# Attention's output with the values as weights, in a two-layer hybrid transformer step on one core

## The chip, the core and the metric

The kernel runs on one core of one Trainium2 chip, written instruction by instruction in Bass: TensorE multiplies, VectorE, ScalarE and GpSimd work beside it, and SyncE issues nearly all the DMA transfers. The metric is the device time of one execution, in microseconds (us). In the profile PE is TensorE's matmul, PEld its weight load, DVE VectorE, ACT ScalarE, POOL GpSimd, and SP or SPq SyncE and its queue. A matmul has two operands: the one that lies in the array (the weights, its columns become the partitions of the result) and the one that streams through it (its columns become the columns of the result). The result lies in PSUM, here in eight banks of 128 partitions by 512 fp32 numbers, ps0 to ps7.

## What is computed

Two layers work on 128 context tokens (b = 0) and 128 latent tokens (b = 1). This case changes only the attention's last step. Cut to what matters:

```python
# D_MODEL 1024, 8 query heads over 2 key/value heads (R = 4), head_dim 64
def one_block(qblk):
    s = jnp.einsum('bqgrd,bkgd->bgrqk', qblk, k).astype(jnp.float32) * scale
    p = jax.nn.softmax(s, axis=-1).astype(v.dtype)
    return jnp.einsum('bgrqk,bkgd->bqgrd', p, v)
...
# latent tokens: k, v = 128 cached keys and 128 own; context tokens: 128 own keys
x = x + gt1 * (jnp.concatenate([att, ml], axis=-1) @ w_out)
...
x = x + gt2 * _moe(h, ...)        # 16 experts, top 2, gate/up/down of 1024 x 512
```

The softmax's division is done last: the kernel computes the sum of exp(score) times value, and divides by the sum of exp(score) of the row.

## The kernel before

All weights (some 289 MB of traffic) are streamed from HBM once, in loads of 2 MB, into ten places in SBUF: a ring of seven, two places called `beside` and one called `over`. SyncE issues them in one written order, and each load waits until the instruction that read the place's last contents is done. In each layer TensorE's program is: norm and projections (L764, L778), the transposes of keys and queries, scores, the parallel mLSTM heads, attention, the output projection in four quarters `mix` 0 to 3 (L1014), the router, and eight pairs of experts (`into_hidden` L1100, `down` L1130), 64 matmul instructions in each of three blocks of a pair.

The order on each engine is the order of the code. A PSUM bank is handed on by a plan, `bank_plan`: every result has a key, `begin(key)` makes TensorE wait until the bank's last contents were read, `full(engine, key)` makes a reader wait until the result is there, and `free(key)` tells that it was read. Attention's results take banks 4, 5 and 6 in turn, in the order in which they are listed; `shiftdot` (a small product for the router, L994) comes into bank 5 behind them.

The steps around the change, in each layer:

- TensorE's weighted sums, L969 (b = 1, over cached keys and own keys) and L976 (b = 0). The exponentials (`pT1`, `pT0`, keys on partitions, 128 queries as columns) are the weights, and the values `cv` and `vx` stream, 64 numbers and a 1 behind them: so the 65th column is the divisor, on the same partition as its query. Bank keys `o10`, `o11`, `o00`, `o01`.
- VectorE's `attended(b)`: a reciprocal of the four divisors of a half (L1840) and a multiplication of 128x256 (L1841) into `on`, twice for each b.
- TensorE's mLSTM state products (L984, keys `C`), a transpose of the state's n (L990), `shiftdot` (L994), then `turn_heads` (L909), eight transposes that turn the attention output so that the heads' columns lie on partitions, and eight of the mLSTM output (L1002, keys `mlT`). ScalarE copies the turned heads from PSUM into `cat` (L1487), the operand of the output projection.
- VectorE between them: `heads_out(1)` ends with L1810, then `attended(1)`, the output gate's product (L1869, two of 128x512), `attended(0)`, the head norm's product (L1874, two of 128x512; `ml_ready`, for which L1002 waits), and the copy of n (L1877).
- SyncE: the first two loads into `beside` wait for key `o01`. The first into `over` waits until the layer's states are written out, the last of them a small transfer from L1877's copy.
- GpSimd loads the next layer's state and cache when `o11` is there.

Of the kernel before, what the change touches and what calls it, by code (L numbers as in the profile page):

```python
# [22 lines left out]
ALU = mybir.AluOpType  # L23
# [3 lines left out]
P = 128  # L27
# [105 lines left out]
def bank_plan():  # L133
# [17 lines left out]
    for l in range(DEPTH):  # L151
# [33 lines left out]
        for k in ("qT1", "kT1", "qT0", "kT0", "s10", "s11", "s12", "s13", "s00", "s01",  # L185
                  "p10", "p11", "p12", "p13", "p00", "p01", "o10", "o11", "o00", "o01", "oT1", "oT0"):
            att(k)
# [85 lines left out]
def build(nc, t):  # L273
    banks, weights = bank_plan(), weight_plan()
    with ExitStack() as ctx:
# [26 lines left out]
        cv = sb("cv", [P, NKV, HD + 1])  # L302
        vx = sb("vx", [P, NB, NKV, HD + 1])
# [4 lines left out]
        shares = sb("shares", [P, NB, NQ])  # L308
# [40 lines left out]
        on = qkr[:, :, 0:NQ * HD]  # L349
# [146 lines left out]
        def _(sp):  # L496
# [56 lines left out]
            for l in range(DEPTH):  # L553
# [57 lines left out]
        def _(pe):  # L611
# [121 lines left out]
            for l in range(DEPTH):  # L733
# [170 lines left out]
                def turn_heads(b):  # L904

                    bank = begin((f"oT{b}", l))
                    taken(pe, (f"o{b}0", l), (f"o{b}1", l))
                    for j in range(4):
                        mm = pe.transpose(bank[:, j * P:(j + 1) * P], on[:, b, j * P:(j + 1) * P], ident)  # L909
                    done((f"oT{b}", l), mm)  # L910
# [51 lines left out]
                for g in range(NKV):  # L962
                    bank = begin((f"o1{g}", l))
                    taken(pe, (f"p1{2 * g}", l), (f"p1{2 * g + 1}", l))
                    for n in range(4):
                        j, par = n // 2, n % 2
                        for kb in range(2):
                            v = cv[:, g, :] if kb == 0 else vx[:, 1, g, :]
                            mm = pe.matmul(bank[:, n * (HD + 1):(n + 1) * (HD + 1)], pT1[:, 2 * g + par, j, kb, :], v,  # L969
                                           start=(kb == 0), stop=(kb == 1))  # L970
                    done((f"o1{g}", l), mm)
                taken(pe, ("p00", l), ("p01", l))
                for g in range(NKV):
                    bank = begin((f"o0{g}", l))
                    for n in range(4):
                        mm = pe.matmul(bank[:, n * (HD + 1):(n + 1) * (HD + 1)], pT0[:, n % 2, 2 * g + n // 2, :], vx[:, 0, g, :],  # L976
                                       start=True, stop=True)
                    done((f"o0{g}", l), mm)
# [17 lines left out]
                turn_heads(1)  # L996
                turn_heads(0)
# [6 lines left out]
                taken(pe, ("oT1", l), ("oT0", l))  # L1004
# [270 lines left out]
        def _(act):  # L1275
# [69 lines left out]
            for l in range(DEPTH):  # L1345
# [138 lines left out]
                for b in (1, 0):  # L1484
                    key = (f"oT{b}", l)
                    bank = full(act, key)
                    act.activation(cat[:, 0:4, b * P:(b + 1) * P], bank[:, :].rearrange("p (k t) -> p k t", k=4),  # L1487
                                   ACT.Copy).then_inc(free(key), 1)
# [75 lines left out]
        def _(dve):  # L1564
# [4 lines left out]
            dve.memset(vx[:, :, :, HD:], 1.0)  # L1569
            dve.memset(cv[:, :, HD:], 1.0)  # L1570
# [87 lines left out]
            for l in range(DEPTH):  # L1658
# [87 lines left out]
                for b in range(NB):  # L1746
# [3 lines left out]
                    dve.tensor_copy(vx[:, b, :, 0:HD], bank[:, NKV * HD:2 * NKV * HD].rearrange("p (g d) -> p g d", g=NKV))\  # L1750
# [83 lines left out]
                def attended(b):  # L1834

                    for g in range(NKV):
# [4 lines left out]
                        dve.tensor_tensor(on[:, b, 4 * g * HD:4 * (g + 1) * HD].rearrange("p (n d) -> p n d", n=4), o[:, :, 0:HD],  # L1841
                                          per_col(share, HD), ALU.mult).then_inc(free(key), 1)
# [207 lines left out]
        def _(pool):  # L2050
            def layer_loads(l):
                pool.dma_start(C0[:, :, 0:MD], t["state_C"][0, l].rearrange("a h d e -> d (a h) e")).then_inc(layer_in, 16)
                pool.dma_start(ck[:, :], t["cache_k"][0, l].rearrange("s g d -> s (g d)")).then_inc(layer_in, 16)
                pool.dma_start(cv[:, :, 0:HD], t["cache_v"][0, l]).then_inc(layer_in, 16)
# [6 lines left out]
            def pool_keys(l):  # L2061
# [3 lines left out]
                pool.dma_start(t["new_cache_v"][0, l], vx[:, 0, :, 0:HD]).then_inc(kv_out, 16)  # L2065
# [18 lines left out]
            for l in range(DEPTH):  # L2084
# [21 lines left out]
                if l + 1 < DEPTH:  # L2106
                    full(pool, ("o11", l))
# [53 lines left out]
```

## Time and profile before

| | |
|---|---|
| median of 3 runs | 792.96 us (792.9 to 793.29) |
| profiled execution, its own time | 794.9 us |
| its span | 793.0 us |
| TensorE busy | 759.5 us, 96% of the span |
| VectorE, ScalarE, GpSimd busy | 329.3, 158.2, 56.6 us |
| mean of the DMA | 365 GB/s |

The span is the time from the first to the last instruction in the trace; the execution's own time has about 1.9 us around it. A busy TensorE is one with an instruction in flight, not one at its peak.

### The profile page before, as it was taken

The numbers are of one execution on the slowest core, as the hardware profiler recorded it, in microseconds if no ns is written. First come the engines' busy times: TensorE is split into PE (matmuls) and PEld (weight loads), VectorE is DVE, ScalarE is ACT, GpSimd is POOL, SyncE is SP. The second block draws the span as 40 slices with busy tenths as digits, with TensorE's granted clock in tenths as the row PEclk, the third lists the DMA queues.
The fourth block names the chain that finished last, engine by engine and source line by source line (L and its number), as shares of the span: only waits on it lengthen the run. The fifth ranks groups of instructions, "written<-read, shape, count | busy, mean of one in ns | idle before, by whom it ended". The sixth has DMA issues, their size and how long they took to land.

```text
span 793.0 us, 10913 instructions
## 1 busy us (share of the span) xinstructions
PE 759.5 (96%) x4683; PEld 401.3 (51%) x4683; DVE 329.3 (42%) x534; ACT 158.2 (20%) x355; POOL 56.6 (7%) x69
## 2 busy tenths in 40 slices
PE   3799999999999999999899999999899999999997
PEld 2265556786534433444245646688653444344423
DVE  0279566714323232123228965772431323213223
ACT  2301114602212012020012111361221201102001
POOL 0040052101100000000000004200110000000000
PEclk9999999999999999999999999999999999999999
DMA  8999907999999999999999970579889999999993
GB/s 346 403 378 374 375 7 295 413 362 424 426 420 424 423 421 425 426 419 423 422 407 407 380 301 0 218 289 397 326 328 400 427 426 418 424 426 419 426 421 152
DMA packets 49858, 289.41 MB, mean 365 GB/s; under 512 B 3401, under 2 KB 5761, under 8 KB 23697
## 3 DMA queue, kind: packets, MB, share of 16 engines
q1 hardware_dynamic: 48080, 285.30, 88.6%
q0 software_dynamic: 1488, 3.31, 1.2%
q8 instruction: 39, 0.64, 0.3%
q10 hardware_dynamic: 240, 0.08, 0.0%
q14 instruction: 11, 0.08, 0.0%
HBM read 286.31 MB, written 2.37 MB: 364 GB/s over the span
## 4 chain that ended last, share of the span: by engine, by line
PE 83%; DMA 13%; DVE 2%; SPq 1%; ACT 1%; issue 0%; ACTq 0%; DVEq 0%
PE ps L1100 22%; PE ps L764 16%; PE ps L1130 12%; DMA ring<-in_w_e_up 9%; PE ps L1014 7%; PE ps L1084 4%; DMA ring<-in_w_in 4%; PE ps L778 4%; PE ps L639 3%; PE ps L1145 2%; PE ps L1112 1%; PE ps L1155 1%; PE ps L892 1%; PE ps L917 1%; PE ps L947 1%; DVE xT L1654 1%
## 5 line engine op out<-in xcount | busy, mean ns | idle before, releaser
L1100 PE MATMUL ps<-ring,xe 128*64 128x512 f32 x688 | 151.8, 594 | 4.0 <-DMA ring<-in_w_e_up 4.0
L764 PE MATMUL ps<-ring,hT 128*128 128x512 f32 (+1 forms) x320 | 128.7, 564 | 2.0 <-DMA ring<-in_w_in 2.0
L1100 PEld LDWEIGHTS ps<-ring,xe 128*64 128x64 f32 x688 | 48.5, 137 | 105.3 <-issue 99.8
L764 PEld LDWEIGHTS ps<-ring,hT 128*128 128x128 f32 x320 | 62.1, 196 | 65.2 <-issue 59.5
L1130 PE MATMUL ps<-ring,ex 128*32 128x512 f32 x736 | 92.0, 594 | 0.2 <-issue 0.2
L1995 DVE COPY ye<-ps 64x512 f32<-64x512 f32 (+1 forms) x28 | 19.3, 689 | 164.2 <-PE ps L1130 164.1
L1014 PE MATMUL ps<-hT,ring 128*128 128x256 f32 x256 | 57.1, 381 | 0.0
L1979 DVE RECIPROCAL ex<-ex 128x512 f32<-128x512 f32 x16 | 53.6, 3353 | 0.6
L1130 PEld LDWEIGHTS ps<-ring,ex 128*32 128x32 f32 x736 | 26.0, 110 | 52.1 <-issue 49.4
L1977 DVE TENSOR_SCALAR ex<-ex 128x512 f32<-128x512 f32 x16 | 6.8, 427 | 109.4 <-ACT ex L1528 109.4
L1014 PEld LDWEIGHTS ps<-hT,ring 128*128 128x128 f32 x256 | 48.0, 190 | 7.2 <-issue 0.8
L1100 PE MATMUL ps<-beside,xe 128*64 128x512 f32 x208 | 46.2, 594 | 0.0
L1528 ACT ACTIVATE ex<-ps 128x512 f32<-128x512 f32 x16 | 9.6, 597 | 143.4 <-PE ps L1100 143.4
L1130 PE MATMUL ps<-beside,ex 128*32 128x512 f32 x224 | 35.3, 594 | 2.0 <-issue 2.0
L1678 DVE SCALAR_TENSOR_TENSOR pT<-ring,cT,pT 128x2048 f32<-128x2048 f32 x14 | 32.9, 2348 | 5.6 <-DMA ring<-in_w_mod 5.6
L1678 DVE SCALAR_TENSOR_TENSOR sideways<-ring,cT,sideways 128x2048 f32<-128x2048 f32 x14 | 32.9, 2347 | 0.0
L1084 PEld LDWEIGHTS ps<-lists,hT 128*128 128x128 f32 x256 | 29.7, 192 | 5.8 <-issue 4.9
L639 PE MATMUL ps<-ring,cT 128*32 128x512 f32 (+1 forms) x320 | 31.6, 525 | 0.6 <-DMA ring<-in_w_mod 0.6
L1084 PE MATMUL ps<-lists,hT 128*128 128x128 f32 x256 | 31.6, 278 | 0.1
L1544 ACT ACTIVATE ye<-ps 64x512 f32<-64x512 f32 (+1 forms) x28 | 16.6, 592 | 68.7 <-PE ps L1130 68.6
L1521 ACT ACTIVATE xe<-ps 128x512 f32<-128x512 f32 x32 | 19.1, 597 | 54.0 <-PE ps L1084 54.0
L1100 PEld LDWEIGHTS ps<-beside,xe 128*64 128x64 f32 x208 | 14.6, 137 | 30.0 <-issue 29.9
(272 smaller groups left out, 803.6 us busy)
## 6 DMA issues: line engine op xcount, KB each, us to landing
ring<-in_w_mod SPq DMA_DIRECT2D x24, 2048.0 KB, 19.1
ring<-in_w_e_up SPq DMA_DIRECT2D x23, 2048.0 KB, 20.0
ring<-in_w_e_gate SPq DMA_DIRECT2D x20, 2048.0 KB, 22.3
ring<-in_w_e_down SPq DMA_DIRECT2D x19, 2048.0 KB, 23.2
ring<-in_w_in SPq DMA_DIRECT2D x10, 2048.0 KB, 23.4
beside<-in_w_e_gate SPq DMA_DIRECT2D x8, 2048.0 KB, 25.5
beside<-in_w_e_down SPq DMA_DIRECT2D x7, 2048.0 KB, 19.8
beside<-in_w_e_up SPq DMA_DIRECT2D x5, 2048.0 KB, 18.1
```

The lines of the kernel that those rows point to most:

```text
L639: mm = pe.matmul(bank[32 * g:32 * g + 32, 0:width], cT[:, c:c + 32], w[:, k, g * width:(g + 1) * width], start=(c == 0), stop=(c == NB * ( ...
L764: mm = pe.matmul(bank[:, 0:width], hT[:, k, b * P:(b + 1) * P], w[:, k, :], start=(k == 0), stop=(k == KD - 1))
L778: mm = pe.matmul(bank[:, j * TOK:(j + 1) * TOK], w[:, k, h * MD:(h + 1) * MD], hT[:, k, :], start=(k == 0), stop=(k == KD - 1))
L1014: mm = pe.matmul(bank[:, j * TOK:(j + 1) * TOK], w[:, k, c:c + P], cat[:, k, :], start=(k == 0), stop=(k == KD - 1))
L1084: mm = pe.matmul(bank[:, c:c + P], htok[:, b, 2 * i + k, :], pick[:, b, 4 * q:4 * q + 4, :].rearrange("p e c -> p (e c)"), start=True, sto ...
L1100: mm = pe.matmul(bank[PLACES * j:PLACES * j + PLACES, :], xe[:, k, c:c + PLACES], w[:, j, i, :], start=(k == 0), stop=(k == KD - 1))
L1130: mm = pe.matmul(bank[32 * g:32 * g + 32, :], hidT[:, k, c:c + SLOTS], w[j][:, k, half * 512:(half + 1) * 512], start=(k == 0), stop=(k == ...
L1521: act.activation(xe[:, 2 * i:2 * i + 2, :].rearrange("p k (e b s) -> p b (k e) s", e=4, b=NB), bank[:, :].rearrange("p (b n s) -> p b n s" ...
L1544: ins = act.activation(ye[r, plane, 0:512], bank[r, :], ACT.Copy)
L1678: ins = dve.scalar_tensor_tensor(modsum[b], w[:, k % 2, :], one, modsum[b], ALU.mult, ALU.add)
L1979: dve.reciprocal(ex[:, :], ex[:, :]).then_inc(silu_step, 1)
L1995: ins = dve.tensor_copy(ye[r, plane, 512:1024], bank[r, :])
```

## The change

For each b and each of the two key/value heads the values are now the weights (64 columns) and the exponentials of two query heads stream (256 columns). The result has the head's 64 numbers on partitions and the queries as columns, which is the form that `cat` wants. Even query heads go to partitions 0 to 63 and odd ones to 64 to 127. The same products with ones instead of values give the divisors, the same number on all 64 partitions, in a second bank (`d1`, `d0`). The divisors are therefore 128x512 numbers where they were 128x4 four times over (two of these reciprocals for each b). The transposes `turn_heads` and their banks go, with ScalarE's two copies. VectorE multiplies from PSUM straight into `cat`. `attended(0)` moves behind the head norm's product.

```diff
-                  "p10", ... "p01", "o10", "o11", "o00", "o01", "oT1", "oT0"):
+                  "p10", ... "p01", "o1", "d1", "o0", "d0"):
...
-                                full(sp, ("o01", l))
+                                full(sp, ("d0", l))
...
+                def over_keys(key, blocks, parts):
+                    bank = begin((key, l))
+                    for g in range(NKV):
+                        for i, part in enumerate(parts):
+                            for par in range(2):
+                                v = blocks[i][:, g, :] if blocks else ones[:, 0:HD]
+                                mm = pe.matmul(bank[64 * par:64 * par + 64, g * TOK:(g + 1) * TOK], v, part(g, par),
+                                               start=(i == 0), stop=(i == len(parts) - 1))
+                    done((key, l), mm)
...
+                over_keys("o1", (cv, vx[:, 1]), both)
+                over_keys("d1", None, both)
                 taken(pe, ("p00", l), ("p01", l))
+                over_keys("o0", (vx[:, 0],), own_keys)
...                                     # the state products C
+                over_keys("d0", None, own_keys)
                 filling(6, 7)
...                                     # nT, shiftdot
-                turn_heads(1)
-                turn_heads(0)
...
 def attended(b):
-                    for g in range(NKV):
-                        key = (f"o{b}{g}", l)
-                        o = full(dve, key)[:, 0:4 * (HD + 1)].rearrange("p (n d) -> p n d", n=4)
-                        share = shares[:, b, 4 * g:4 * g + 4]
-                        step(dve.reciprocal(share, o[:, :, HD]))
-                        dve.tensor_tensor(on[...], o[:, :, 0:HD], per_col(share, HD), ALU.mult).then_inc(free(key), 1)
+                    key = (f"d{b}", l)
+                    bank = full(dve, key)
+                    dve.reciprocal(share[:, b, :], bank[:, :]).then_inc(free(key), 1)
+                    taken(dve, key)
+                    key = (f"o{b}", l)
+                    bank = full(dve, key)
+                    dve.tensor_tensor(cat[:, 0:4, b * P:(b + 1) * P], bank[:, :].rearrange("p (k t) -> p k t", k=4),
+                                      share[:, b, :].rearrange("p (k t) -> p k t", k=4), ALU.mult).then_inc(free(key), 1)
...
                 for b in range(NB):
                     note(dve.tensor_tensor(o[b], o[b], mqT[:, b, :, :], ALU.mult))
-                attended(0)
                 dve.wait_ge(head_rstd, l + 1)
                 settle()
                 for b in range(NB):
                     dve.tensor_tensor(o[b], o[b], per_col(hr[:, b, :], MD), ALU.mult).then_inc(ml_ready, 1)
+                attended(0)
```

Three places of the program follow, the same in both layers. A row is one instruction or a run of equal ones (x3): line, operation, result and operands, size of the result, and the semaphores it waits for (one fp32 matmul here is two instructions in the trace); `bank_read5` is "the last contents of bank 5 were read", `bank_full5` "the result in bank 5 is there". Lines are those of each kernel's own file.

TensorE before, the end of the weighted sums: the last products of b = 1 (`cv` cached, `vx` own values, streaming) and all those of b = 0.

```order
L969 MATMUL ps6<-cv,pT1 128x65
L969 MATMUL ps6<-vx,pT1 128x65
L976 MATMUL ps4<-vx,sideways 128x65 [waits bank_read4,bank_read6]
L976 MATMUL ps4<-vx,sideways 128x65 x3
L976 MATMUL ps5<-vx,sideways 128x65 [waits bank_read5]
L976 MATMUL ps5<-vx,sideways 128x65 x3
```

TensorE now, all but one of the new groups: `o1` in ps5, `d1` in ps6 (with `ones`), `o0` in ps4.

```order
L910 MATMUL ps5<-pT1,cv 64x256 [waits bank_read4,bank_read6,bank_read5,bank_read1,bank_read0]
L910 MATMUL ps5<-pT1,cv 64x256
L910 MATMUL ps5<-pT1,vx 64x256 x2
L910 MATMUL ps5<-pT1,cv 64x256 x2
L910 MATMUL ps5<-pT1,vx 64x256 x2
L910 MATMUL ps6<-pT1,ones 64x256 [waits bank_read6]
L910 MATMUL ps6<-pT1,ones 64x256 x7
L910 MATMUL ps4<-sideways,vx 64x256 [waits bank_read4,bank_read6]
L910 MATMUL ps4<-sideways,vx 64x256 x3
```

Sixteen products of 128x65 and eight behind them became eight, eight and four of 64x256.

TensorE before, from the last of the state products to the transposes of the mLSTM output; `wr,modc` is `shiftdot`, `cst,qkr` the turned heads, `cst,og` the mLSTM output.

```order
L984 MATMUL ps1<-mv,kw 128x129 [waits bank_read1]
L984 MATMUL ps1<-mv,kw 128x129
L990 MATMUL ps2<-cst,qk 8x128 [waits bank_read1,bank_read2]
L994 MATMUL ps5<-wr,modc 2x16 [waits bank_read5]
L994 MATMUL ps5<-wr,modc 2x16 x7
L909 MATMUL ps6<-cst,qkr 128x128 [waits bank_read6,bank_read5]
L909 MATMUL ps6<-cst,qkr 128x128 x3
L909 MATMUL ps4<-cst,qkr 128x128 [waits bank_read5,bank_read4]
L909 MATMUL ps4<-cst,qkr 128x128 x3
L1002 MATMUL ps3<-cst,og 128x128 [waits ml_ready,bank_read3]
L1002 MATMUL ps3<-cst,og 128x128 x3
```

TensorE now, at the same place.

```order
L976 MATMUL ps1<-mv,kw 128x129 [waits bank_read1]
L976 MATMUL ps1<-mv,kw 128x129
L910 MATMUL ps5<-sideways,ones 64x256 [waits bank_read5]
L910 MATMUL ps5<-sideways,ones 64x256 x3
L983 MATMUL ps2<-cst,qk 8x128 [waits bank_read1,bank_read2]
L987 MATMUL ps5<-wr,modc 2x16 [waits bank_read5]
L987 MATMUL ps5<-wr,modc 2x16 x7
L993 MATMUL ps3<-cst,og 128x128 [waits ml_ready,bank_read3]
L993 MATMUL ps3<-cst,og 128x128 x3
L993 MATMUL ps0<-cst,og 128x128 [waits ml_ready,bank_read0]
L993 MATMUL ps0<-cst,og 128x128 x3
```

The eight transposes are gone. `d0` has come in behind the state products and needs bank 5 read, whose contents are now `o1`; `shiftdot` needs bank 5 read as before, and its contents are now `d0`.

VectorE before, from the end of the mLSTM's sum to the product for which the transposes of `og` wait.

```order
L1840 RECIPROCAL shares<-ps5 128x4 [waits bank_full5]
L1841 TENSOR_TENSOR qkr<-ps5,shares 128x256 [waits dve_step]
L1840 RECIPROCAL shares<-ps6 128x4 [waits bank_full6]
L1841 TENSOR_TENSOR qkr<-ps6,shares 128x256 [waits dve_step]
L1869 TENSOR_TENSOR og<-og,mqT 128x512 [waits head_sum]
L1869 TENSOR_TENSOR og<-og,mqT 128x512
L1840 RECIPROCAL shares<-ps4 128x4 [waits bank_full4]
L1841 TENSOR_TENSOR qkr<-ps4,shares 128x256 [waits dve_step]
L1840 RECIPROCAL shares<-ps5 128x4 [waits bank_full5]
L1841 TENSOR_TENSOR qkr<-ps5,shares 128x256 [waits dve_step]
L1874 TENSOR_TENSOR og<-og,hr 128x512 [waits dve_step,head_rstd]
```

VectorE now, at the same place; `qkr` is where the reciprocals `share` lie, `hT` is `cat`.

```order
L1822 RECIPROCAL qkr<-ps6 128x512 [waits bank_full6]
L1826 TENSOR_TENSOR hT<-ps5,qkr 128x4x128 [waits bank_full5,bank_read6]
L1854 TENSOR_TENSOR og<-og,mqT 128x512 [waits head_sum]
L1854 TENSOR_TENSOR og<-og,mqT 128x512
L1858 TENSOR_TENSOR og<-og,hr 128x512 [waits dve_step,head_rstd]
L1858 TENSOR_TENSOR og<-og,hr 128x512
L1822 RECIPROCAL qkr<-ps5 128x512 [waits bank_full5]
L1826 TENSOR_TENSOR hT<-ps4,qkr 128x4x128 [waits bank_full4,bank_read5]
L1862 COPY nst<-ps2 8x128 [waits bank_full2]
```

Four pairs of a small reciprocal and a multiplication became two pairs of 128x512, and the second pair now stands behind both products with `hr`. Bank 5 as `shiftdot` needs it (`d0` read) is given by the second 128x512 reciprocal.

## Rows read from the trace of the kernel before

**Rows 1.** The page: shares of the last chain, two groups of instructions

```profile
PE 83%; DMA 13%; DVE 2%; SPq 1%; ACT 1%; issue 0%; ACTq 0%; DVEq 0%
L1100 PE MATMUL ps<-ring,xe 128*64 128x512 f32 x688 | 151.8, 594 | 4.0 <-DMA ring<-in_w_e_up 4.0
L1979 DVE RECIPROCAL ex<-ex 128x512 f32<-128x512 f32 x16 | 53.6, 3353 | 0.6
```

**Rows 2.** Stretch, length, busy of PE, PEld, DVE, ACT, POOL; PEclk, DMA share, GB/s

```profile
170.00:175.00 5.00, 5.00 (x30) 4.01 (x29) 1.13 (x4) 0.63 (x1) 0.00 (x0) 1.00 0.74 298
530.00:535.00 5.00, 4.43 (x50) 3.97 (x49) 3.08 (x9) 2.90 (x9) 1.47 (x2) 1.00 0.77 267
585.00:590.00 5.00, 5.00 (x26) 1.71 (x24) 0.00 (x0) 0.02 (x1) 0.00 (x0) 1.00 0.51 164
610.00:730.00 120.00, 120.00 (x786) 51.33 (x786) 31.32 (x28) 18.38 (x32) 0.00 (x0) 1.00 1.01 423
```

**Rows 3.** SyncE's timeline: start, us to the last issue, what

```profile
174.13 0.37 SPq L579 DMA_DIRECT2D over<-in_w_e_up  x1
...
175.06 12.89 SPq L584 DMA_DIRECT2D ring<-in_w_e_down  x2
193.74 2.78 SPq L579 DMA_DIRECT2D ring<-in_w_e_gate  x2
...
530.16 0.37 SPq L579 DMA_DIRECT2D beside<-in_w_e_gate  x1
...
586.54 0.34 SPq L584 DMA_DIRECT2D ring<-in_w_e_down  x1
```

**Rows 4.** The chain in order of time, around the change: start, us, what

```profile
147.47 3.52 PE ps L969 x32
150.99 1.79 PE ps L976 x16
152.77 1.85 PE ps L984 x16
...
155.45 0.48 PE ps L994 x16
155.93 1.03 PE ps L909 x8
156.96 0.87 PE ps L1002 x8
157.83 7.06 PE ps L1014 x32
...
532.75 0.48 PE ps L994 x16
```

**Rows 5.** The same chain, stretches that give rates of TensorE

```profile
34.14 15.70 PE ps L764 x32
...
65.86 27.66 PE ps L764 x64
...
231.47 13.88 PE ps L1100 x64
```

**Rows 6.** VectorE's timeline around attended: start, us, what

```profile
150.09 0.69 DVE L1810 TENSOR_TENSOR mqT<-work 128x512 f32<-128x512 f32 x1
...
150.91 0.42 DVE L1841 TENSOR_TENSOR qkr<-ps,shares 128x256 f32<-128x256 f32 x1
...
151.80 1.28 DVE L1869 TENSOR_TENSOR og<-og,mqT 128x512 f32<-128x512 f32 x2
...
154.10 1.28 DVE L1874 TENSOR_TENSOR og<-og,hr 128x512 f32<-128x512 f32 x2
...
528.28 0.18 DVE L1840 RECIPROCAL shares<-ps 128x4 f32<-128x4 f32 x1
```

**Rows 7.** Two stretches of 2 us before and in a slow clock

```profile
32.00:34.00 2.00, 0.15 (x1) 0.00 (x0) 1.96 (x5) 1.36 (x5) 0.00 (x0) 1.00 1.05 432
...
36.00:38.00 2.00, 2.00 (x3) 0.72 (x3) 0.00 (x0) 0.00 (x0) 0.00 (x0) 0.50 1.00 392
```

More of the change, by code:

```diff
@@ L185, in bank_plan @@
         for k in ("qT1", "kT1", "qT0", "kT0", "s10", "s11", "s12", "s13", "s00", "s01",
-                  "p10", "p11", "p12", "p13", "p00", "p01", "o10", "o11", "o00", "o01", "oT1", "oT0"):
+                  "p10", "p11", "p12", "p13", "p00", "p01", "o1", "d1", "o0", "d0"):
             att(k)
@@ L301, in build @@
         ck = sb("ck", [P, NKV * HD])
-        cv = sb("cv", [P, NKV, HD + 1])
-        vx = sb("vx", [P, NB, NKV, HD + 1])
+        cv = sb("cv", [P, NKV, HD])
+        vx = sb("vx", [P, NB, NKV, HD])
         rstd = sb("rstd", [P, TOK])
@@ L307, in build @@
         peaks = sb("peaks", [P, NB, NQ])
-        shares = sb("shares", [P, NB, NQ])
         dn = sb("dn", [P, NB, MH, 2])
@@ L348, in build @@
         gl = prob[:, 18 * P:20 * P]
-        on = qkr[:, :, 0:NQ * HD]
+        share = qkr[:, :, 0:NQ * HD]
         inter_s = hT.ap().rearrange("p k t -> p (k t)")[:, MH * TOK:MH * TOK + 6 * (MD + 1)].rearrange("p (n d e) -> p n d e", n=3, d=2)
@@ L902, in carried @@
                     done((("inter", h), l), mm)
[L904 to L910, printed above, removed]
+                def over_keys(key, blocks, parts):
[7 more added lines that the diff above has]
+                    done((key, l), mm)
                 def cross_scores(i):
@@ L961, in _ @@
                 taken(pe, (("akv", 0), l), (("akv", 1), l))
-                for g in range(NKV):
[L963 to L971, printed above, removed]
-                taken(pe, ("p00", l), ("p01", l))
[L973 to L978, printed above, removed]
+                both = [lambda g, par, kb=kb: pT1[:, 2 * g + par, :, kb, :] for kb in range(2)]
+                own_keys = [lambda g, par: pT0[:, par, 2 * g:2 * g + 2, :]]
+                taken(pe, *[(f"p1{i}", l) for i in range(4)])
+                over_keys("o1", (cv, vx[:, 1]), both)
+                over_keys("d1", None, both)
+                taken(pe, ("p00", l), ("p01", l))
+                over_keys("o0", (vx[:, 0],), own_keys)
                 pe.wait_ge(kw_ready, 2 * (l + 1))
@@ L1003, in _ @@
                     done((("mlT", b), l), mm)
-                taken(pe, ("oT1", l), ("oT0", l))
+                taken(pe, ("o1", l), ("o0", l))
                 fill = last_section(l)
@@ L1483, in _ @@
                                    bank[:, 0:2 * (MD + 1)].rearrange("p (d e) -> p d e", d=2), ACT.Copy).then_inc(free(key), 1)
[L1484 to L1488, printed above, removed]
                 key = (("mlT", 0), l)
@@ L1749, in _ @@
                     dve.tensor_copy(qk[:, b, NQ * HD:], bank[:, 0:NKV * HD])
-                    dve.tensor_copy(vx[:, b, :, 0:HD], bank[:, NKV * HD:2 * NKV * HD].rearrange("p (g d) -> p g d", g=NKV))\
+                    dve.tensor_copy(vx[:, b, :, :], bank[:, NKV * HD:2 * NKV * HD].rearrange("p (g d) -> p g d", g=NKV))\
                         .then_inc(free(key), 1)
@@ L1834, in attended @@
                 def attended(b):
-                    for g in range(NKV):
-                        key = (f"o{b}{g}", l)
-                        o = full(dve, key)[:, 0:4 * (HD + 1)].rearrange("p (n d) -> p n d", n=4)
-                        share = shares[:, b, 4 * g:4 * g + 4]
-                        step(dve.reciprocal(share, o[:, :, HD]))
-                        dve.tensor_tensor(on[:, b, 4 * g * HD:4 * (g + 1) * HD].rearrange("p (n d) -> p n d", n=4), o[:, :, 0:HD],
-                                          per_col(share, HD), ALU.mult).then_inc(free(key), 1)
+                    key = (f"d{b}", l)
[6 more added lines that the diff above has]
+                                      share[:, b, :].rearrange("p (k t) -> p k t", k=4), ALU.mult).then_inc(free(key), 1)
                 dve.wait_ge(layer_in, 16 * LAYER_LOADS * (l + 1))
@@ L2053, in layer_loads @@
                 pool.dma_start(ck[:, :], t["cache_k"][0, l].rearrange("s g d -> s (g d)")).then_inc(layer_in, 16)
-                pool.dma_start(cv[:, :, 0:HD], t["cache_v"][0, l]).then_inc(layer_in, 16)
+                pool.dma_start(cv[:, :, :], t["cache_v"][0, l]).then_inc(layer_in, 16)
             def gate_weights(l):
@@ L2106, in _ @@
                 if l + 1 < DEPTH:
-                    full(pool, ("o11", l))
+                    full(pool, ("o1", l))
                     full(pool, (("inter", MH - 1), l))
```

4 lines of the change are left out of this document (1 added, 3 removed).

## The prediction, made before the changed kernel had run

> **What bounds the kernel now.** I read the chain of work that ended last first, because a busy share is no bound. Its shares are 83% TensorE and 13% DMA, and the reader should see that the two alternate: the DMA comes in at the end of each layer's experts, and the group of L1100 waited 4.0 us in all for `e_up` weights [rows 1]. So I looked at the DMA's stretches. From 610 to 730 us, in the experts, it moves 423 GB/s at a share of 1.01: full, and a load of 2.1 MB takes 2.1 / 423 = 4.96 us there. Where it is not full is what decides: 0.74 from 170 to 175 us, 0.77 from 530 to 535, 0.51 from 585 to 590 [rows 2]. SyncE's timeline says why: loads are issued in order when a place comes free, and those at 193.74 and 586.54 us waited for TensorE's own progress [rows 3]. A TensorE that comes later to the output projection issues these loads later by as much, and from there to the layer's end the DMA has no pause in which to catch up. Both bounds therefore move with TensorE's lateness in this stretch, and the question is only when the output projection (L1014) starts: at 157.83 us in layer 0 [rows 4].
>
> **What ends the wait there.** In the chain around the change there is hardly an idle time: weighted sums 3.52 and 1.79 us, state products 1.85, `shiftdot` at 155.45, turned heads 1.03, mLSTM output 0.87 [rows 4]. VectorE runs beside it, close behind: `heads_out(1)` starts its last instruction at 150.09 and takes 0.69, a multiplication of 128x256 takes 0.42, the two products with the gate 1.28 and the two with the norm 1.28 [rows 6]. It has no slack of microseconds to give.
>
> **TensorE's own work.** Removed per layer: 3.52 + 1.79 + 1.03 = 6.34 us [rows 4]. Added: 8 + 8 + 4 + 4 products of 64x256. The trace has none of this form. The nearest is L1100, 64-column weights in alternating halves of the array: 64 instructions of 512 columns in 13.88 us, 0.217 each, against 27.66 for 64 full-width ones, 0.432 [rows 5]. Half the columns gives 0.108; a product is two instructions, so 24 x 0.217 = 5.2 us. The other bound is that the halves don't overlap: 0.441, from L1014's 7.06 us for 16 products of 256 columns [rows 4], or 10.6 us. The new products alternate halves just as L1100 does, so I take 5.2: TensorE saves 1.1 us per layer in work.
>
> **VectorE's work.** Removed per layer: four multiplications of 0.42 and four small reciprocals of 0.18 [rows 6], 2.4 us. Added: two reciprocals of 128x512 and two multiplications of 128x512. The reciprocal of that size takes 3353 ns [rows 1]; the multiplication 0.64, half of 1.28 [rows 6]. That is 8.0 us. The row reads SBUF and the new one PSUM; the small reciprocals from PSUM show no penalty at 0.18, so I keep 3.35. The Trainium skill ("VectorE: DVE Perf Modes", "First, the fixed hardware budget") says a reciprocal iterates with a repeat count of 8; at the clock of 0.96 GHz that the page gives, 512 x 8 cycles would be an estimated 4.3 us, and the stalls below would be 3.7 us longer in all. The measured 3353 ns speaks against it, though for another source.
>
> **The new wait, layer 0.** o1 and d1 are 16 products: from 147.47, 3.5 us, so d1 is there at about 151.2 with the end of its pipeline, and VectorE, done at 150.8, waits until then. Then in its order: reciprocal 3.35, multiplication 0.64, gate 1.28, norm 1.28, reciprocal 3.35, in sum 9.9, to 161.1 us. `shiftdot` needs bank 5, now held by d0 until that second reciprocal has read it. So it starts at 161.1 instead of 155.45: 5.65 late. Behind it on TensorE stand the mLSTM transposes and the output projection, without the turned heads' 1.03: 4.6 us late. Before that TensorE also waits some 1.6 us for bank 5 ahead of d0 (o1 is read at 155.2; o0 and the state products end near 153.7); this is inside the 4.6, not added to it. The order of VectorE that puts the norm ahead of `attended(0)` gives nothing back, because the mLSTM transposes stand behind `shiftdot`. `over`'s first load, which waits for L1877's copy and a transfer [rows 3], is behind the same reciprocal, but the next layer's state is loaded 1.7 us earlier (o1 ends earlier than the last of L969); I count nothing.
>
> **Layer 1.** Here VectorE came to `attended(1)` at 528.28 [rows 6] and d1 is there at the same time: TensorE's way from the sums to `shiftdot` is 8.0 us in layer 0, so here it began at 524.8 or before and has d1 by 528.5. 528.28 + 9.9 = 538.2, against `shiftdot` at 532.75 [rows 4]: 5.45, less 1.03, 4.4 us late. The first load into `beside`, at 530.16 [rows 3], goes to d0's end, some 3 us later, and the DMA stands idle so much longer; but it was idle again from 585 to 590 [rows 2] for a load that waits on TensorE, so those 3 us are inside TensorE's lateness.
>
> **The clock.** From 32 to 34 us TensorE was busy 0.15 of 2 us, and from 36 to 38 us its granted clock is 0.50, the 1.2 GHz level [rows 7]; the first 32 instructions behind that pause took 15.70 us where 32 take 13.83 [rows 5]: 1.87 us lost. The new stalls leave it nearly idle for 6.3 of 7.4 us (153.7 to 161.1). I therefore expect a fall in both layers. Its price is at least what falls on the dense output projection, 1.9; it may take the eight transposes too (0.87 [rows 4], doubled), giving 2.8. I take 2.0 per layer, near the measured pause. The Trainium skill ("TensorE: Matmul & The Clock Gate", "What you observe") states the same rule, that activity releases the throttle and a pause brings it back; by it alone the sum has these 4.0 us, without it 4.0 less.
>
> **What hides some of it.** In layer 0 the DMA has a short queue when `e_gate` is issued at 193.74. Three loads were issued by 175.1 [rows 3], the DMA was dry shortly before (0.74 [rows 2]) and starts on them near 176; with 3 x 4.96 they end at 190.9, and the one issued at 187.95 (175.06 + 12.89) ends at 195.9. From issue to bytes a load needs at least 1.0 us (issued at 530.16 into an idle DMA, and the share of 530 to 535 is 0.77, so bytes flow from 531.2 or later [rows 2, 3]). So 193.74 was early by 1.2 us at most. That is all the cover; I take 0.5.
>
> **The sum.** Layer 0: 4.6 + 2.0 - 0.5 = 6.1. Layer 1: 4.4 + 2.0 = 6.4. Together 12.5 us on the profiled execution's 794.9, which is 1.9 above the median of 793.0: **805.5 us**.
>
> **The rivals.**
> - *No fall of the clock.* The few products inside the stall keep it up; short pauses elsewhere cost nothing. Then 8.5 us: 801.5. Against it: rows 7, with a shorter pause. 0.17.
> - *The stream hides it.* TensorE waited 4.0 us for `e_up` [rows 1], so up to 2 us per layer of lateness could be free: 801.5 with the fall, 797.5 without. It needs loads that don't wait for TensorE, and rows 3 has them waiting at both places. 0.08.
> - *The halves don't overlap.* 16 products for o1 and d1 take 7.1 instead of 3.5, VectorE starts 3.5 later in layer 0 and 3 in layer 1: 812. 0.06.
> - *The skill's slow reciprocal*, 4.3 us: 809. 0.03.
> - *Faster.* The 128x512 reciprocal is cheap. The lateness is two reciprocals less what went, 2r - 2.0 in layer 0 and 2r - 2.2 in layer 1; at r = 1.0 us it is nothing, and at the multiplication's 0.64 TensorE's 1.1 us of saved work counts: 791. For it: nothing but that the row has another source. 0.04, with the no change near r = 1.
> - My forecast: 0.62.
>
> **Numbers.** 800.5 to 810 leaves out the faster case, half of the stream's, the halves' and some of the tails, some 0.18. A measurement of this kernel tells 0.2%, 1.6 us, from nothing. Slower by more: all but the last rival and a little of the second, 0.95; same 0.02; faster 0.03.
>
> **What would show it.** Right: a wait of TensorE of over 4 us before the 2x16 products of `shiftdot`, ended by VectorE's reciprocal of 128x512 from PSUM at 3.3 us; the output projection starting 4.5 to 8 us after 157.83; a granted clock of 0.5 just behind the stall in both layers; the load after 193.74 late by as much; the chain passing through VectorE in both layers. Wrong: a reciprocal under 2 us, a clock that stays at 1.00, or pauses before the last pair's weights shrinking by more than 1 us per layer.

## The result, and the profile after

The changed kernel takes **805.03 us** (median of 4 runs, 803.31 to 807.03) against 792.93 for the kernel before on the same chip: a ratio of 1.0151, interval 1.0135 to 1.0168. It is 12.1 us slower, where 12.5 was forecast. Its profiled execution took 803.31 us, with a span of 801.5.

The first lines are the page of the changed kernel: busy times, then the chain that ended last.

```profile
PE 756.4 (94%) x4660; PEld 395.7 (49%) x4667; DVE 341.2 (43%) x524; ACT 155.7 (19%) x351; POOL 55.9 (7%) x69
...
PE 81%; DMA 12%; DVE 4%; SPq 1%; issue 1%; ACT 1%; DVEq 0%; ACTq 0%
```

TensorE is busy 3 us less than before and the kernel is slower: it waits more. (Those 3 us are no measure of the work saved. Slow stretches of the clock count in them, and the two profiles have theirs in different places.) VectorE's share of the chain is 4%, against 2% before, and TensorE's 81%, against 83% [rows 1]. Where VectorE came in is seen in the chain of layer 0's stretch of the change (start us, us, what; "x" counts instructions).

```profile
144.70 3.63 PE ps L910 x32
...
148.35 3.37 DVE qkr L1822
...
151.74 0.69 DVE hT L1826
152.44 1.21 DVE og L1854 x2
...
154.35 0.68 DVE og L1858
155.03 3.28 DVE qkr L1822
...
158.36 0.59 PE ps L987 x16
158.94 1.90 PE ps L993 x8
160.84 7.42 PE ps L1005 x32
```

Read against [rows 4], where nearly every step was TensorE's: from the end of the products for o1 and d1 (148.33) to `shiftdot` (L987, 158.36) every step is VectorE's, but for some 0.6 us of short gaps between them. Its two reciprocals of 128x512 (L1822) make 6.65 of the 10.0 us. Layer 1 has the same tail:

```profile
531.24 3.36 DVE qkr L1822
...
537.91 3.28 DVE qkr L1822
...
541.23 0.59 PE ps L987 x16
541.82 1.90 PE ps L993 x8
```

TensorE's own timeline shows the two waits in brackets, with what ended each:

```profile
152.49 1.08 PE L910 MATMUL ps<-sideways,ones 128*64 128x256 f32 x8 [1.34 <-DVE hT L1826]
...
158.36 0.59 PE L987 MATMUL ps<-wr,modc 128*2 128x16 f32 x16 [4.58 <-DVE qkr L1822]
```

The clock is in the windows (us, then busy us of PE, PEld, DVE, ACT, POOL, the granted clock, the DMA's share, GB/s):

```profile
154.00:156.00 2.00, 0.00 (x0) 0.00 (x0) 2.00 (x3) 0.00 (x0) 0.00 (x0) 0.73 0.99 369
156.00:158.00 2.00, 0.00 (x0) 0.00 (x0) 2.00 (x1) 0.00 (x0) 0.00 (x0) 0.50 1.03 399
158.00:160.00 2.00, 1.64 (x22) 1.59 (x23) 1.18 (x3) 0.00 (x0) 0.64 (x1) 0.50 1.01 422
160.00:162.00 2.00, 2.00 (x8) 1.79 (x8) 1.12 (x4) 1.63 (x5) 0.80 (x2) 0.56 1.01 422
162.00:164.00 2.00, 2.00 (x12) 1.74 (x11) 0.01 (x1) 0.00 (x0) 0.00 (x0) 1.00 1.01 420
...
538.00:540.00 2.00, 0.00 (x0) 0.00 (x0) 2.00 (x1) 0.00 (x0) 0.00 (x0) 0.50 0.99 311
540.00:542.00 2.00, 0.77 (x17) 0.71 (x18) 1.97 (x3) 0.00 (x0) 0.00 (x0) 0.50 0.97 410
542.00:544.00 2.00, 2.00 (x10) 1.91 (x10) 0.34 (x2) 1.10 (x5) 0.51 (x1) 0.50 1.03 434
544.00:546.00 2.00, 2.00 (x11) 1.77 (x10) 0.88 (x4) 0.32 (x2) 0.00 (x0) 0.99 0.99 422
```

The idle TensorE falls to the 1.2 GHz level in both layers and stays there through the small products behind the wait. In layer 0 it keeps that level into the output projection, whose first quarter takes 7.42 us; in layer 1 only to its first instructions (7.13 us). The load behind that projection is late too. It is issued at 197.11 (SyncE's timeline; its equal before at 193.74 [rows 3]), which is 6.1 us late, not 3.4, when both are counted from the same point, as below:

```profile
197.11 0.38 SPq L578 DMA_DIRECT2D ring<-in_w_e_gate  x1
```

**How spans are compared.** The profile of before had a clock fall of its own at 96 to 100 us, in the first layer's projections (granted 0.70 and 0.50), which this one has not. The chains of before and of the changed kernel show its price for the same 64 instructions, 1.7 us:

```profile
96.57 22.52 PE ps L764 x64
95.49 20.84 PE ps L763 x64
```

Another 1.1 us between the two had come up ahead of that. So every time after it is 2.8 us ahead of before's: the first product `mv,W` of the parallel heads starts at 128.05, before's at 130.81. I therefore measure from that product, in each layer, and call the time from it to the output projection's first product the *way*. (In layer 1 the same product starts it.)

| us | way, layer 0 | to the next norm's sums | to TensorE's first work of layer 1 | way, layer 1 | to the next norm's sums | to the last transposes |
|---|---|---|---|---|---|---|
| before | 26.94 | 57.27 | 282.78 | 25.40 | 55.52 | 276.47 |
| after | 32.59 | 63.40 | 288.65 | 30.90 | 61.21 | 282.00 |
| difference | 5.65 | 6.13 | 5.87 | 5.50 | 5.69 | 5.53 |

5.87 for layer 0 and 5.53 for layer 1 make 11.4 of the 12.1 us. All the loss is there when TensorE reaches the norm behind the output projection; what is given back behind it (0.3 and 0.2) is no more than such stretches differ from run to run.

### The profile page after: what moved, and what is told of

Its sections match the earlier page's. It is cut to its first block, busy times and chain, and to the rows that moved or that the text cites. A ratio compares the mean times of both kernels' runs of the same rounds, so it can differ in the third digit from the quotient of the medians.

```text
span 801.5 us, 10860 instructions
## 1 busy us (share of the span) xinstructions
PE 756.4 (94%) x4660; PEld 395.7 (49%) x4667; DVE 341.2 (43%) x524; ACT 155.7 (19%) x351; POOL 55.9 (7%) x69
## 3 DMA queue, kind: packets, MB, share of 16 engines
HBM read 286.31 MB, written 2.37 MB: 360 GB/s over the span
## 4 chain that ended last, share of the span: by engine, by line
PE 81%; DMA 12%; DVE 4%; SPq 1%; issue 1%; ACT 1%; DVEq 0%; ACTq 0%
PE ps L1091 22%; PE ps L763 16%; PE ps L1121 12%; DMA ring<-in_w_e_up 9%; PE ps L1005 7%; PE ps L1075 4%; PE ps L777 3%; PE ps L638 3%; DMA ring<-in_w_mod 3%; PE ps L1136 2%; DVE qkr L1822 2%; PE ps L1103 1%; PE ps L1146 1%; PE ps L891 1%; PE ps L690 1%
## 5 line engine op out<-in xcount | busy, mean ns | idle before, releaser
L763 PE MATMUL ps<-ring,hT 128*128 128x512 f32 (+1 forms) x320 | 125.3, 551 | 0.0
L763 PEld LDWEIGHTS ps<-ring,hT 128*128 128x128 f32 x320 | 60.2, 190 | 61.4 <-issue 58.2
```

What stands on the lines that cost most here:

```text
L763: mm = pe.matmul(bank[:, 0:width], hT[:, k, b * P:(b + 1) * P], w[:, k, :], start=(k == 0), stop=(k == KD - 1))
```

## The experiments

The theory: two reciprocals of 3.35 us hold bank 5, TensorE comes late by some 4.6 us and the clock falls on top; what is late there is late at the end. The rivals are those of the prediction: no price for the clock, a DMA stream that hides the lateness, halves that don't overlap. The kernels below ran in three groups on one chip each; the ratio is to the kernel before in the same group.

| label | median us | before | ratio (95%) |
|---|---|---|---|
| e1_flat | 792.1 | 792.75 | 0.9992 (0.998 to 1.0003) |
| e2_warm | 804.44 | 792.75 | 1.0148 (1.0125 to 1.0171) |
| e3_late0 | 798.41 | 792.75 | 1.0073 (1.0049 to 1.0098) |
| e4_late1 | 798.31 | 792.75 | 1.0065 (1.0044 to 1.0086) |
| e5_bank6 | 804.09 | 793.05 | 1.0135 (1.0113 to 1.0156) |
| e6_order | 805.03 | 793.05 | 1.0144 (1.0123 to 1.0165) |
| e7_beside | 792.6 | 793.05 | 0.9996 (0.9986 to 1.0007) |
| e8_scalar | 790.9 | 793.05 | 0.9979 (0.9967 to 0.9991) |
| e9_bank6_warm | 800.13 | 792.56 | 1.0103 (1.0087 to 1.0118) |
| e10_after | 804.58 | 792.56 | 1.0156 (1.0142 to 1.017) |
| e11_scalar2 | 789.22 | 792.56 | 0.9962 (0.9948 to 0.9975) |
| e12_halves | 792.44 | 792.56 | 0.9998 (0.9989 to 1.0007) |

### Without the reciprocals

```diff
-                    dve.reciprocal(share[:, b, :], bank[:, :]).then_inc(free(key), 1)
+                    dve.tensor_scalar(share[:, b, :], bank[:, :], 0.0, 0.3, ALU.mult, ALU.add).then_inc(free(key), 1)
```

> The changed kernel with the two 128x512 reciprocals of each layer replaced by a cheap operation of the same shape from the same bank into the same place (a constant 0.3 comes out, so attention's output is not divided by its sums). Theory (two reciprocals of 3.35 us each stand ahead of the read of bank 5, which shiftdot needs): the lateness per layer is two times the cheap operation's 0.7 us less 2.0 to 2.2, so the output projection starts 0.6 to 1 us earlier than in the kernel before, the clock stays at 1.00 there, and the time is 790.5 to 792.5 us. Rival A (the new products, their banks or SyncE's later wait for beside cost the time): 800 us or more. Rival B (only part is the reciprocals): 795 to 800.

Measured: 792.1 us; the whole loss is gone (with a constant in place of 1/d, so attention's output is left undivided). The two instructions take 0.70 us in the chain, in the same places:

```profile
148.37 0.70 DVE qkr L1822
...
152.30 0.70 DVE qkr L1822
...
154.62 6.91 PE ps L1005 x32
```

The ways are 26.39 and 24.70, 0.55 and 0.70 shorter than before's, and the clock stays at 1.00. So the products, their banks, the new waits and the missing transposes cost nothing; the reciprocals' length is the one cause. It also bears on the halves: had they not overlapped, this kernel would be slow too.

### The clock kept up through the wait

```diff
+                warm((("mlT", 0), l), 22)
                 bank = begin(("shiftdot", l))
```

`warm` is 22 matmuls of zeros into a bank that nobody reads yet (L690).

> The changed kernel with 22 matmuls of 128x512 in bf16 on zeros (some 4.8 us of work, into a bank that is free) ahead of shiftdot, where TensorE waits 4.6 us. Theory (the pause lets the clock fall, and that costs 1.2 to 1.5 us per layer in slow transposes and a slow begin of the output projection): granted clock 1.00 from there on, the eight transposes back at 0.9 us instead of 1.9, time 801.8 to 803 us. Rival (the fall costs nothing, all is VectorE's): 805 or more, as the added matmuls end a little after the stall.

Measured: 804.44 us (801.77 to 805.41), which the times can't tell from the changed kernel: less than expected, and as a test by the times it failed. The trace tells more. The granted clock is 1.00 throughout, and the chain shows what the same steps cost at that level:

```profile
153.45 4.76 PE ps L690 x21
158.21 0.48 PE ps L988 x16
158.69 1.02 PE ps L994 x8
159.71 6.91 PE ps L1006 x32
```

From `shiftdot` to the end of the first quarter this is 8.41 us; the changed kernel's 0.59, 1.90 and 7.42 make 9.91. At the next norm's sums it is 1.26 us ahead in layer 0 (62.14 against 63.40) and 0.97 in layer 1 (60.24 against 61.21). The ways are 31.88 and 30.20, which is 4.94 and 4.80 over before's. A part of that is the experiment's own: the added matmuls end a little after VectorE has freed bank 5 (its second reciprocal, then `shiftdot`):

```profile
154.56 3.35 DVE L1823 RECIPROCAL qkr<-ps 128x512 f32<-128x512 f32 x1
158.14 0.55 PE L988 MATMUL ps<-wr,modc 128*2 128x16 f32 x16
```

Behind the heads' first product, `shiftdot` starts at 30.47 us in layer 0 and 28.79 in layer 1, in the changed kernel at 30.31 and 28.62. Without that 0.2 us the stall alone, with the clock up, is 4.8 and 4.6, and the clock's part at the norm's sums is 1.4 and 1.1 us. At the end of each layer less of it can be seen: e2 is 0.95 ahead when layer 1 starts (287.70 against 288.65) and 0.49 at the last transposes (281.51 against 282.00). The times tell still less. The trace is of the fastest of the four runs, the only one with a mean granted clock of 1.000; the three others (803.6 to 805.4 us) have 0.997, and no trace shows where theirs fell.

### The lateness alone, in the kernel before

```diff
                 taken(pe, ("oT1", l), ("oT0", l))
+                if l == 0:
+                    warm((("mix", 0), l), 22)
```

and the same with `l == 1`: 4.76 us more ahead of the output projection in one layer, and nothing else.

> The kernel before with 22 matmuls of 128x512 in bf16 on zeros (4.8 us) ahead of the output projection, in layer 0 alone: a lateness of TensorE of known size. Theory (the weight stream waits for TensorE's progress and covers only 0.5 to 1.2 us): +3.6 to +4.3 us, 796.5 to 797.3. Rival (the stream's waits before the last pair, some 4 us, hide most of it in layer 0): +0.5 to +2.5, 793.5 to 795.5.

> The same 22 matmuls ahead of the output projection in layer 1 alone. Theory (no cover at all in layer 1, where the stream is dry between 585 and 590 us): +4.7 to +4.9 us, 797.6 to 797.9. Rival (the stream hides up to the 2 us that TensorE waits before the last pair): +2.7 to +3.5, 795.6 to 796.5.

Measured: 798.41 and 798.31 us, 5.7 and 5.6 over before. In the traces both lengthen the way by 4.80 (31.74 and 30.20). In layer 1 the last transposes come 5.05 later. In layer 0 3.9 of the 4.8 are left when layer 1 starts (286.67 against 282.78), but 4.4 at the heads' first product in layer 1 (383.28 against 378.83), and kernels that do the same up to there (e4, and e7 but for its loads) are 0.2 to 0.7 us from before over such a stretch. So by the trace 0.4 to 0.9 us of layer 0's lateness is hidden, hardly more than that spread, and by the times none; nothing is hidden in layer 1. The rival by which the stream hides the lateness is out for both. The expectations, 796.5 to 797.3 and 797.6 to 797.9, were a little low; the traces fit them better than the times. (In e3's profiled run 3.0 us of its own time lie outside the span, 1.8 to 1.9 in the others; why is open.)

### The bank of `shiftdot`

```diff
-        put(("shiftdot", l), 5)
+        put(("shiftdot", l), 6)
```

Now `shiftdot` and the mLSTM transposes run inside the wait; the output projection still needs `cat` from the second reciprocal.

> The changed kernel with shiftdot in bank 6 (read early) instead of bank 5, so that shiftdot and the eight transposes of the mLSTM output no longer wait for the second reciprocal; the output projection still waits for o0 times that reciprocal. Theory: it starts when the multiplication behind the reciprocal ends, 0.7 us after the reciprocal, instead of 0.59 + 1.90 us after it, so 1.8 us per layer are gained, time 801 to 802 us. Rival (bank 5 was the cost itself, the projection could start once it is free): 794 to 797. Rival (nothing hangs on the bank): 805.

Measured: 804.09 us, a miss. The way became 1.5 us shorter, near the 1.8 that were expected (31.07 and 29.39), but the projection gave it back:

```profile
158.84 0.82 issue
159.66 8.83 PE ps L1005 x32
```

The 0.82 us without a name are those of VectorE's multiplication into `cat`, which runs from 158.87 to 159.56. The projection's first quarter takes 8.83 us where the changed kernel needs 7.42 and a warm one 6.91, with a granted clock of 0.55 from 160 to 162 us and 0.60 from 162 to 164. TensorE is idle for 3.32 us before the projection, the fall comes later, and all of it lands on dense products. To tell whether that is the reason, 15 warm matmuls were put behind the transposes of this kernel:

```diff
+                warm((("mix", 0), l), 15)
                 taken(pe, ("o1", l), ("o0", l))
```

> shiftdot in bank 6 (as in the kernel tried before) and 15 matmuls of 128x512 in bf16 on zeros (3.25 us) in the wait ahead of the output projection. In the trace of the one without them the wait fell ahead of the projection, and the clock fell onto its dense products: from its start to the next norm 32.0 us in layer 0 instead of 30.3. Theory (the bank's 1.5 us per layer were gained and lost again to the clock): with the clock held at 1.00, 30.3 and 30.1 us for these stretches, and from the mLSTM's first product to the norm 61.3 and 59.4 us (63.4 and 61.2 in the changed kernel): 801 to 802.5 us. Rival (the bank gains nothing): 804 to 805.

Measured: 800.13 us, 4.45 less than the unedited changed kernel in the same group (e10), and a little below the 801 to 802.5 expected. The first quarter (its chain) is back at its rate, behind the same start:

```profile
155.49 3.23 PE ps L690 x14
...
158.76 7.14 PE ps L1006 x32
```

The next norm's sums come at 61.41 and 59.50, 1.7 earlier than in e5 and 2.0 and 1.7 earlier than in the changed kernel. The two parts need each other: warmth alone gave 1.3 and 1.0, the bank alone 0.3 and 0.0.

### VectorE's order, and SyncE's wait

```diff
+                attended(0)
                 dve.wait_ge(head_rstd, l + 1)
...
-                attended(0)
```

> The changed kernel with VectorE's old order: attended(0) ahead of the head norm's product again. Theory: the second reciprocal ends 1.3 us earlier, but the transposes then wait for the norm's product behind it, so only 0.2 to 0.6 us per layer are gained: 803.8 to 804.7 us. Rival (the new order is what helps, as the transposes' operand comes earlier): slower than the changed kernel, 807 or more. Rival (the new order is the cause of the loss): 800 or less.

Measured: 805.03 us, no difference that can be told. The ways are 0.45 shorter (32.14 and 30.45), which is gone again at the norm's sums (63.48 and 61.22). The clock falls here too, and later than in the changed kernel: it is at 0.50 from 160 to 164 us and still at 0.74 from 164 to 166, when the projection runs. VectorE's order is not a cause. In the kernel before, the loads into `beside` were then made to wait longer, about as the change has them wait:

```diff
                             if slot in BESIDE:
-                                full(sp, ("o01", l))
+                                full(sp, (("C", MH - 1), l))
+                                full(sp, ("oT1", l))
```

> The kernel before with SyncE's wait for the loads into beside put behind the state products and the first turned heads (some 3.8 us later in layer 1, 4 us in layer 0), nothing else changed: the changed kernel's later wait alone. Theory (the DMA is dry for that longer in layer 1, but dry again later on TensorE's progress): no change, 792.5 to 793.5. Rival (the DMA's lost time comes back at the end): 796 to 797.

Measured: 792.6 us, no change. The later loads are no cause either.

### The reciprocals on ScalarE

ScalarE is busy 19% of the time. There 1/d is exp(-ln d), two instructions; d1 is computed ahead of o1, and `shiftdot` has bank 6.

```diff
+                def divided(b):
...
+                    act.activation(share[:, b, :], bank[:, :], ACT.Ln).then_inc(free(key), 1)
+                    taken(act, key)
+                    act.activation(share[:, b, :], share[:, b, :], ACT.Exp, scale=-1.0).then_inc(share_ready, 1)
...
-                    dve.reciprocal(share[:, b, :], bank[:, :]).then_inc(free(key), 1)
-                    taken(dve, key)
+                    dve.wait_ge(share_ready, NB * l + 2 - b)
```

> The changed kernel with the reciprocals taken off VectorE: ScalarE makes them as exp(-ln(d)), two operations of 0.6 us of 128x512, in its pause before the squares of b = 1 and behind the state's copies; d1 is multiplied ahead of o1 and takes bank 5, shiftdot bank 6. Theory (VectorE's 6.7 us per layer were the loss, TensorE's own work is 1.1 us less than before): the output projection starts about 1 us earlier than in the kernel before, 790 to 792 us, faster than both. Rival (ScalarE becomes the bound, its copies of the state end later and hold up nT): 793 to 796.

Measured: 790.9 us, ratio 0.9979 (0.9967 to 0.9991): in the range that was expected, and faster than the kernel before by 0.2%, little more than such a measurement tells. ScalarE's timeline:

```profile
146.47 0.60 ACT L1467 ACTIVATE qkr<-ps 128x512 f32<-128x512 f32 x1 [0.55 <-PE ps L910]
147.10 0.63 ACT L1469 ACTIVATE qkr<-qkr 128x512 f32<-128x512 f32 x1
...
152.05 0.60 ACT L1467 ACTIVATE qkr<-ps 128x512 f32<-128x512 f32 x1 [0.63 <-PE ps L910]
152.68 0.63 ACT L1469 ACTIVATE qkr<-qkr 128x512 f32<-128x512 f32 x1
```

1.23 us for what takes VectorE 3.36. VectorE is no step of TensorE's chain any more; what is left is a gap of 0.42 us ahead of the projection, where its multiplication into `cat` ends (154.04, the projection starts at 154.14). The ways are 26.25 and 24.20, 0.69 and 1.20 shorter than before's, and the new form's saving of TensorE's work shows at last. The Trainium skill ("ScalarE: Activation LUTs", "What it computes") sends a reciprocal to VectorE, because of the accuracy of ScalarE's own function for it; the pair of ln and exp is another way round, and here the faster by 2.1 us each. How accurate it is was not measured.

A second version puts d0 ahead of the state products and `divided(0)` ahead of ScalarE's copies of them, and the transpose of n behind those of the mLSTM output:

```diff
                 over_keys("o0", (vx[:, 0],), own_keys)
+                over_keys("d0", None, own_keys)
...
-                over_keys("d0", None, own_keys)
                 filling(6, 7)
...
+                divided(0)
                 act.wait_ge(kv_out, 32 * (l + 1))
```

> The kernel with ScalarE's reciprocals, rearranged: d0's products ahead of the state products, ScalarE's reciprocal of d0 ahead of its copies of the state, and the transpose of n behind those of the mLSTM output. Theory (in layer 1 the output projection waited 0.4 us for the multiplication behind ScalarE's second reciprocal, and shiftdot for ScalarE's copies; in layer 0 the weight stream is the bound, so nothing is gained there): 0.5 to 1.0 us less than without it, 789.9 to 790.6. Rival (the states are written out later and the load into over with them, the DMA's pause in layer 0 grows): 791 to 793.

Measured: 789.22 us, ratio 0.9962, the fastest of all and somewhat better than expected. The ways are 25.41 and 23.36. As expected, the time saved in layer 0 is not kept: there the ways of e8 and e11 are 0.7 and 1.5 us shorter than before's, but layer 1 starts at 282.95 and 282.83, no earlier than before's 282.78. In layer 1 the last transposes come at 274.91 and 273.93 against 276.47, so all of the gain is made there. A lateness in layer 0 costs nearly its length (e3); a lead gives nothing. Its chain from the sums to the projection is one block of TensorE's work, with no gap:

```profile
144.55 5.33 PE ps L910 x48
149.88 1.98 PE ps L977 x16
151.86 0.48 PE ps L983 x16
152.34 1.02 PE ps L989 x8
153.37 0.11 PE ps L993
153.48 6.91 PE ps L1004 x32
```

### The halves

e8 with the products of one half in a row, as the outermost loop, instead of in turn:

```diff
-                    for g in range(NKV):
-                        for i, part in enumerate(parts):
-                            for par in range(2):
+                    for par in range(2):
+                        for g in range(NKV):
+                            for i, part in enumerate(parts):
```

> The kernel with ScalarE's reciprocals (first form), with all products for partitions 0 to 63 ahead of all those for 64 to 127, so that neighbours use the same half of the array. Theory (only alternating halves overlap, as in the experts' products): the 24 products of a layer take 10.6 us instead of 5.2 and stand on TensorE's path: +10 us on 790.9, 800 to 801.5. Rival (64 columns of weights go at this rate in any order): 791.

Measured: 792.44 us, where 800 and more was expected: my theory of it fell, and the rival's 791 came near. Against e8 the ways are 1.05 and 1.04 longer, no more (27.30 and 25.24). The 40 instructions of d1, o1 and o0 take 5.49 us instead of 4.47 (chains of layer 1), where 40 that don't overlap would take 8.6 at the projection's rate (6.91 us for 32). TensorE's timeline in layer 0 shows why:

```profile
145.29 2.21 PE L910 MATMUL ps<-pT,ones 128*64 128x256 f32 x13
147.13 0.43 PE L910 MATMUL ps<-pT,cv 128*64 128x256 f32 x1
147.34 0.38 PE L910 MATMUL ps<-pT,ones 128*64 128x256 f32 x1
147.40 0.38 PE L910 MATMUL ps<-pT,cv 128*64 128x256 f32 x1
```

The products of the next group (`cv`), written behind all of d1's (`ones`), start between the last of these: one half works on d1 while the other is already at o1. I read from it that the order costs only the ends of the run and not the overlap; no other length of run was tried.

### The changed kernel again

> The changed kernel as it is, beside the others on the same chip, so that differences of 1 to 3 us among its variants can be read. All theories: 804 to 806 us. In its trace: a granted clock of 0.5 for 7 us around the second reciprocal in both layers, wherever the fall begins.

Measured: 804.58 us, ratio 1.0156, for comparison within the last group. The clock falls again, with 0.69, 0.50, 0.50 and 0.60 in the four windows from 156 to 164 us.

## Why the prediction came out right, step by step

- **What bounds it.** Right. The chain leaves TensorE for VectorE at one place per layer, and what is lost there is, all but a few tenths, lost at the end: e3 and e4 show that with lateness alone, e1 by taking the cause away.
- **TensorE's work.** 0.108 us per instruction from L1100's rate; 32 took 3.63, so 0.113, and all 48 took 5.33 in e11, so 0.111. Right: against the 6.34 removed the saving is 1.0 us per layer, 1.1 forecast. It shows in e8 and e11, where nothing else stands in the way.
- **The reciprocal.** 3.35 us from SBUF was carried over to PSUM; it measured 3.36 and 3.35. The 4.3 us, estimated from the Trainium skill's repeat count, are too long from either source.
- **The new wait.** Right in its mechanism and nearly in its size. `shiftdot` was forecast 5.65 and 5.45 us late; counted from the heads' first product it is 5.74 late in layer 0 (30.31 against 24.57) and 5.58 in layer 1 (28.62 against 23.04). For the stall at full clock 4.6 and 4.4 were forecast, and e2 leaves 4.8 and 4.6. Of the 0.2 that is missing each time, 0.1 lies in VectorE's hand-overs (10.0 us measured for the 9.9), and 0.07 in the turned heads. They gave back 0.96, not 1.03: from `shiftdot` to the projection it is 2.37 us before and 1.41 in e2. The multiplication into `cat` has no part in it, as it ends at 159.03 and the projection starts at 160.64.
- **The clock.** That it falls, and where, was right. The size was wrong: 2.0 per layer, measured 1.4 and 1.1 at the norm's sums, and 1.5 and 1.2 from `shiftdot` to the end of the projection's first quarter. The term was sized by a pause with dense products right behind it. Here the first microseconds at the low level pass in idle time and in 24 small instructions, which lose 1.0 us (0.59 + 1.90 against 0.48 + 1.02), and the projection only 0.5 (0.2 in layer 1). Where it does stand in front, as in e5, it loses 1.9, as at the pause of [rows 7]. The sentence that the prediction takes from the Trainium skill stands under "What's actually happening" of that page; the trace agrees with it (1.00 from 152 to 154 us, 0.50 from 156 to 160, 1.00 again from 162).
- **The cover.** 0.5 for layer 0 forecast; 0.4 to 0.9 by e3's trace, none by its times, so it is neither shown nor ruled out. In layer 1 none, as forecast.
- **The sum.** 4.8 + 1.4 - 0.3 (5.87 measured) and 4.6 + 1.1 - 0.2 (5.53) in place of 6.1 and 6.4; the 0.3 and 0.2 are what remains, and not measured as cover. The stall was forecast too small by 0.4 us in all and the clock too large by 1.5: 12.5 becomes 11.4. The rest of the 12.1 us, some 0.7, lies between the profiled execution (the fastest of the four) and the median; what it is stays open. So the mechanism was right wherever the runs can tell, but that 12.5 came within 0.4 of the measured number is partly luck: a term too large, one too small, and a rest that no step of the prediction has.
- **The signs.** The wait was 4.58 us, ended by a reciprocal of 3.35. The projection starts at 160.64, only 2.8 us after before's 157.83 as the times stand and 5.65 when counted from the same point; 4.5 to 8 had been asked for. The clock, the load and the chain did as forecast, and the waits for `e_up` weights stayed at 3.8 us (4.0 before).
- **Rivals.** The clock has its price, but it is the small one: by the trace the sum without it is some 9.4 to 9.7 us (8.5 forecast for that rival), by the times e2 and the changed kernel can't be told apart. Halves without overlap, a reciprocal of 4.3 us, a cheap one and a stream that hides the lateness are out.

## What to carry to other kernels

A divisor that is repeated over partitions and columns to save transposes makes its reciprocal 512 columns wide where it was 4, and at 3.35 us that is then the longest step around; cost the widened form by its own row and see what bank it holds meanwhile. Before giving up such a form, ask which idle engine can do the step: with the step on ScalarE the same change is a gain of 0.2%, and of 0.4% in a better order. And when a stall lets the clock fall, look at what runs first behind it: moving the small work ahead of the stall puts the slow stretch on the dense work.

## What the runs showed of the hardware that was not expected

- The granted clock's fall costs by what stands behind it: eight 128x128 transposes took 1.90 us at 0.50 against 1.02 at 1.00 (e2), the first quarter of the projection 8.83 when it stood in front (e5) against 7.42 behind the transposes and 6.91 warm.
- Two 64-column halves of the array overlap across more than neighbours: with eight instructions of one half in a row, 40 took 5.49 us, in turn 4.47, and starts in the trace are out of the written order between the halves (147.13 for `cv`, 147.34 for the `ones` written before it). How far ahead the engine goes was not tried.
- The 128x512 reciprocal takes the same time from PSUM (3.35 us) as from SBUF [rows 1], and ln and exp of the same size on ScalarE 0.60 and 0.63.
